# Reordered bank copies, splits, turns and a root in 8 steps in a hybrid RWKV-7 / gated-DeltaNet block

## What is computed

```python
xn = rmsnorm(x, norm_mix_pre);  p = xn @ w_in      # all projections of both branches
y_a = rwkv7(p);  y_b = gated_delta_rule(p)         # 32 heads of 64, 16 heads of 128, chunks of 64
mixed = sigmoid(p_gate_a) * y_a + sigmoid(p_gate_b) * y_b
x = x + rmsnorm(mixed @ w_out, norm_mix_post)
xn = rmsnorm(x, norm_ffn_pre)
hidden = silu(xn @ ffn_w_gate) * (xn @ ffn_w_up)   # width 5632
return x + rmsnorm(hidden @ ffn_w_down, norm_ffn_post)
```

## Time and profile before

| | us |
|---|---|
| median of 3 runs | 2201.25 (2199.06 to 2201.72) |
| the profiled execution | 2195.88 |
| its span, first to last instruction | 2194.2 |
| PE busy | 2091.8 (95%) |
| PE weight loads busy | 1804.8 (82%) |
| DVE busy | 1427.1 (65%) |
| ACT busy | 1086.2 (50%) |
| POOL busy | 160.2 (7%) |
| mean granted clock of PE | 0.987 |

### The profile page before, as it was taken

How to read it: one execution, slowest core, us unless ns; L and a number is a source line. 1 busy time by engine, 2 the same in 40 slices (tenths; PEclk the granted TensorE clock), 3 DMA queues, 4 the chain that set the end, 5 groups by cost and what they waited for, 6 DMA issues and landing times. The chain is left out here.

```text
span 2194.2 us, 49337 instructions
## 1 busy us (share of the span) xinstructions
PE 2091.8 (95%) x20515; PEld 1804.8 (82%) x20515; DVE 1427.1 (65%) x2868; ACT 1086.2 (50%) x2060; POOL 160.2 (7%) x277
## 2 busy tenths in 40 slices
PE   5999999999999999999999999799999999989997
PEld 5988888888888888888888888678888888878886
DVE  5568777777777877777777785754454444445445
ACT  4555555554655555555465554444444444434443
POOL 3010011011011011101101100000000000000000
PEclk9999999999999999999999999899999999999999
DMA  7655444454545444445454424545555555545553
GB/s 202 170 142 133 124 124 119 125 134 121 135 121 137 126 125 128 119 121 133 125 136 121 128 96 144 177 169 192 189 184 186 188 190 189 174 153 191 191 187 119
DMA packets 386941, 327.28 MB, mean 149 GB/s; under 512 B 11744, under 2 KB 334272, under 8 KB 380352
## 3 DMA queue, kind: packets, MB, share of 16 engines
q1 hardware_dynamic: 372688, 318.53, 49.4%
q10 hardware_dynamic: 14064, 6.04, 1.1%
HBM read 322.44 MB, written 2.10 MB: 148 GB/s over the span
## 5 line engine op out<-in xcount | busy, mean ns | idle before, releaser
L249 PE MATMUL ps<-hi_all,xh 128*128 128x384 f32 (+1 forms) x1568 | 564.1, 360 | 32.0 <-ACT pu L275 29.2
L498 DVE TENSOR_TENSOR lo_all<-stage,hi_all 128x1024 fp32r<-128x1024 f32 x263 | 322.2, 1225 | 365.9 <-ACT hi_all L494 365.6
L251 PE MATMUL ps<-hi_all,xl 128*128 128x384 f32 (+1 forms) x1568 | 531.7, 339 | 0.0
L250 PE MATMUL ps<-lo_all,xh 128*128 128x384 f32 (+1 forms) x1568 | 530.3, 338 | 0.0
L494 ACT ACTIVATE hi_all<-stage 128x1024 fp32r<-128x1024 f32 x260 | 275.5, 1060 | 416.1 <-PE ps L510 415.4
L244 DVE TENSOR_TENSOR lo_all<-stage,hi_all 128x768 fp32r<-128x768 f32 (+1 forms) x400 | 378.0, 965 | 120.2 <-ACT hi_all L239 119.5
L239 ACT ACTIVATE hi_all<-stage 128x768 fp32r<-128x768 f32 (+1 forms) x400 | 327.6, 833 | 216.4 <-PE ps L251 209.8
L249 PEld LDWEIGHTS ps<-hi_all,xh 128*128 128x128 f32 x1568 | 296.4, 189 | 67.9 <-ACT pu L275 36.4
L250 PEld LDWEIGHTS ps<-lo_all,xh 128*128 128x128 f32 x1568 | 297.4, 190 | 0.9
L251 PEld LDWEIGHTS ps<-hi_all,xl 128*128 128x128 f32 x1568 | 296.7, 189 | 0.9
L506 PE MATMUL ps<-hi_all,xh 128*128 128x512 f32 x704 | 277.2, 394 | 3.6 <-DVE lo_all L498 3.4
(11 more groups left out here) (280 smaller groups left out, 2656.8 us busy)
## 6 DMA issues: line engine op xcount, KB each, us to landing
stage<-in_w_in SPq DMA_DIRECT2D x288, 512.0 KB, 5.7
stage<-in_ffn_w_gate SPq DMA_DIRECT2D x44, 1024.0 KB, 5.2
stage<-in_ffn_w_up SPq DMA_DIRECT2D x44, 1024.0 KB, 5.1
stage<-in_ffn_w_down SPq DMA_DIRECT2D x22, 2048.0 KB, 7.4
stage<-in_w_out SPq DMA_DIRECT2D x16, 344.0 KB, 4.2
stage<-in_w_out SPq DMA_DIRECT2D x8, 516.0 KB, 4.9
stage<-in_w_in SPq DMA_DIRECT2D x8, 448.0 KB, 6.9
stage<-in_w_out SPq DMA_DIRECT2D x8, 336.0 KB, 4.0
```

The costliest lines, as they stand in the source:

```text
L249: nc.tensor.matmul(o, xh[:, kc, xs], high, start=kc == 0, stop=False)
L250: nc.tensor.matmul(o, xh[:, kc, xs], low, start=False, stop=False)
L251: return nc.tensor.matmul(o, xl[:, kc, xs], high, start=False, stop=kc == KC - 1)
L498: nc.vector.tensor_tensor(wlo[b], src, whi[b].bitcast(F32), ALU.subtract).then_inc(ffn_lo, 1)
```

## The change

`take_out(act, u, 2)` goes directly behind the copy `rhs` of chunk 2, and the two splits that stood before and after it go behind step (2,2); DVE does one split less ahead of the norms' sums and one more behind step (3,2). At the end of w_out DVE's sums go one ahead of the scales, ACT's first `stage_hi` goes from p = 5 to p = 2, and its `stage_lo` into the next block, behind `new_x(1)`. The first feed-forward block uses three buffers and may split two quanta ahead; PE turns each group one quantum later; the squares of the second norm are done at quanta 6 and 7. Behind the last block PE starts the first down step with bank pair 3, and `hidden`, `turn` and `store` of the last block lie within that step. At the end the banks come in order 2, 3, 1, 0 for both halves, each is squared and weighted by itself, and the results of t = 0 are made between the weighted products of t = 1. `root` replaces `rsqrt` in the feed-forward part: 8 steps, a column at a time, where the factor of each step is a per-partition scalar.

```diff
@@ -118,6 +118,39 @@
...
         step(nc.vector.scalar_tensor_tensor(y, t, 1.5, y, ALU.add, ALU.mult))
+def root_names(tag, columns):
+    return [f"{tag}{k}{c}" for k in ("y", "v", "t0", "z0", "t1", "z1", "t2", "z2") for c in range(columns)]
+def root(nc, dve, done, tag, y, v, w):
+    columns = y.shape[1]
+    def after(name):
+        dve.wait_ge(done.sem, done.after(name))
+    def at(x, c):
+        return x[:, c:c + 1]
+    for c in range(columns):
+        done.step(f"{tag}y{c}", nc.vector.tensor_scalar(at(y, c).bitcast(I32), at(v, c).bitcast(I32), -0.5, 1597463007.0,
+                                                        ALU.mult, ALU.add))
+    for c in range(columns):
+        done.step(f"{tag}v{c}", nc.vector.tensor_scalar(at(w, c), at(v, c), -0.5, None, ALU.mult))
+    for i in range(3):
+        for c in range(columns):
+            after(f"{tag}z{i - 1}{c}" if i else f"{tag}v{c}")
+            done.step(f"{tag}t{i}{c}", nc.vector.scalar_tensor_tensor(at(v, c), at(y, c), at(w, c), at(y, c),
+                                                                      ALU.mult, ALU.mult))
+        for c in range(columns):
+            after(f"{tag}t{i}{c}")
+            done.step(f"{tag}z{i}{c}", nc.vector.scalar_tensor_tensor(at(y, c), at(v, c), 1.5, at(y, c), ALU.add, ALU.mult))
+    for c in range(columns):
+        after(f"{tag}z2{c}")
...
@@ -487,10 +520,10 @@
...
-def stage_hi(act, n, b, src):
-    if not (isinstance(n, int) and n < 2):
-        act.wait_ge(ffn_used, n - 1)
+def stage_hi(act, n, b, src, ahead=1):
+    if not (isinstance(n, int) and n <= ahead):
+        act.wait_ge(ffn_used, n - ahead)
...
@@ -1158,7 +1191,7 @@
...
-def chunk_act(act, u, lag, k, c):
+def chunk_act(act, u, lag, k, c, between=None):
...
@@ -1168,6 +1201,8 @@
...
 fn(f"r{c}", rhs[:], ps[:, 4, 0:CH])
+if between:
+    between()
...
@@ -1265,11 +1300,12 @@
...
 fn("sqq", sq[:, 1:3, :], qkv[:, 0:2, :], ACT.Square)
-fill(1)
-chunk(1, 2)
-take_out(act, u, 2)
-fill(1)
+if prev:
+    chunk_act(act, u, 1, 1, 2, lambda: take_out(act, u, 2))
+else:
+    take_out(act, u, 2)
 chunk(2, 2)
+fill(2)
...
@@ -1351,7 +1387,8 @@
...
 for p in range(OP):
-    if p == OP - 1:
+    if p == 2:
...
@@ -1538,7 +1575,7 @@
...
 chunk(1, 2)
-fill(2)
+fill(1)
...
@@ -1663,8 +1700,9 @@
...
         fill(1)
-    out_scale_dve(dve, p)
-stage_lo(dve, 0, 0, ffn_quantum(0))
+    else:
+        out_scale_dve(dve, p - 1)
+out_scale_dve(dve, OP - 1)
...
@@ -1791,17 +1829,25 @@
...
 down_sum, down_square = sem("down_sum"), sem("down_square")
+B0 = (3, 0, 1, 2)
+LAST_B = (2, 3, 1, 0)
 A = Steps(sem("ffn_act"), [f"hi{g}" for g in G8] + ["ss0", "ss1"])
-V = Steps(sem("ffn_dve"), ["sum", "var"] + rsqrt_names("p") + ["x0", "x1"]
+V = Steps(sem("ffn_dve"), ["sum", "var"] + root_names("p", NT) + ["x0", "x1"]
           + [n for g in G8 for n in ([f"lo{g}", f"x{g + 2}"] if g < 6 else [f"lo{g}"])]
-          + ["v2"] + rsqrt_names("q") + ["half", "gate"]
-          + [n for t in range(NT) for n in [f"w{t}{b}" for b in (3, 2, 0, 1)] + [f"sum{t}", f"var{t}"] + rsqrt_names(f"r{t}_") + [f"y{t}0", f"y{t}1"]])
+          + ["v2"] + root_names("q", NT) + ["half", "gate"]
+          + [f"w0{b}" for b in LAST_B] + ["sum0", "var0"] + root_names("r0_", 1)
+          + ["w12", "y01", "w13", "y00", "w11", "w10", "sum1", "var1"] + root_names("r1_", 1) + ["y11", "y10"])
...
 QE = QD + NB * (JD - 1)
+def split_buffer(q, first):
+    return q % 3 if first else (q + 1) % 2
...
@@ -1830,7 +1876,7 @@
...
 for t in range(NT):
-    for h in range(2):
+    for h in (1, 0):
...
@@ -1853,14 +1899,14 @@
...
         act.wait_ge(ffn_landed[(q // 2) % 4], jb * 32 + 16 * (q // 8 + 1))
-    stage_hi(act, jb * QF + q, q % 2, ffn_quantum(q))
+    stage_hi(act, jb * QF + q, split_buffer(q, first), ffn_quantum(q), 2 if first else 1)
...
     high(q + 1)
-if first and q == 8:
-    for t in range(NT):
+if first and q in (6, 7):
+    for t in (q - 6,):
...
@@ -1879,20 +1925,22 @@
...
     block_act(jb, False)
-store(FB - 1)
-def down_act(j, s, n, landed):
+def down_act(j, s, n, landed, order=range(NB)):
...
         act.wait_ge(ffn_used, n - NB)
+    elif j == 0:
+        act.wait_ge(stored, FB - 1)
...
     act.wait_ge(down_in[s], landed)
-    for b in range(NB):
-        stage_hi(act, n + b, b % 2, down_quantum(s, b))
+    for i, b in enumerate(order):
+        stage_hi(act, n + i, (i + 1) % 2, down_quantum(s, b))
+down_act(0, 0, QD, 16, B0)
+store(FB - 1)
 act.wait_ge(stored, FB)
-for s in range(2):
-    down_act(s, s, QD + NB * s, 16)
+down_act(1, 1, QD + NB, 16)
...
@@ -1900,17 +1948,15 @@
...
 act.wait_ge(down_in[1], 8 * JD)
-for b in (2, 3, 0, 1):
+for b in LAST_B:
     if b < 2:
-        act.wait_ge(ffn_used, QE - 1 + b)
+        act.wait_ge(ffn_used, QE - b)
...
 for t in range(NT):
-    act.wait_ge(down_sum, t + 1)
-    for b in range(NB):
-        if t + b:
-            act.wait_ge(down_square, NB * t + b)
-        if b >= 2:
-            act.wait_ge(V.sem, V.after(f"w{t}{b}"))
+    for i, b in enumerate(LAST_B):
+        act.wait_ge(down_sum, NB * t + i + 1)
+        if t + i:
+            act.wait_ge(down_square, NB * t + i)
...
@@ -1942,7 +1988,7 @@
...
 done("v2")
-rsqrt(nc, dve, V, "q", 0, rr[:], ssx[:], rtm[:])
+root(nc, dve, V, "q", rr[:], ssx[:], rtm[:])
...
@@ -1951,7 +1997,7 @@
...
 if not (first and q == 0):
-    stage_lo(dve, jb * QF + q, q % 2, ffn_quantum(q))
+    stage_lo(dve, jb * QF + q, split_buffer(q, first), ffn_quantum(q))
...
@@ -1973,58 +2019,64 @@
...
 done("var")
-rsqrt(nc, dve, V, "p", 0, rr[:], ssx[:], rtm[:])
+root(nc, dve, V, "p", rr[:], ssx[:], rtm[:])
...
 new_x(1)
+stage_lo(dve, 0, 0, ffn_quantum(0))
...
     block_dve(jb, False)
-dve.wait_ge(gate_done, FB)
-hidden(FB - 1)
...
-def down_dve(j, s, n):
+def down_dve(j, s, n, order=range(NB)):
     left(j, s)
-    for b in range(NB):
-        stage_lo(dve, n + b, b % 2, down_quantum(s, b))
-for s in range(2):
-    down_dve(s, s, QD + NB * s)
+    for i, b in enumerate(order):
+        stage_lo(dve, n + i, (i + 1) % 2, down_quantum(s, b))
+        if isinstance(j, int) and j == 0 and i == 0:
+            dve.wait_ge(gate_done, FB)
+            hidden(FB - 1)
+down_dve(0, 0, QD, B0)
+down_dve(1, 1, QD + NB)
...
 left(JD - 1, 1)
-for i, b in enumerate((2, 3, 0, 1)):
+for i, b in enumerate(LAST_B):
...
+def weighted(t, b):
+    dve.wait_ge(down_square, NB * t + LAST_B.index(b) + 1)
+    cs = slice(CB * b, CB * b + CB)
+    V.step(f"w{t}{b}", nc.vector.tensor_tensor(y2[:, t, cs], ps[:, 2 * b + t, :], row[:, cs], ALU.mult))
+def result(t, h):
+    cs = slice(h * D // 2, (h + 1) * D // 2)
+    V.step(f"y{t}{h}", nc.vector.scalar_tensor_tensor(y2[:, t, cs], y2[:, t, cs], rr[:, t:t + 1], x2[:, t, cs],
+                                                     ALU.mult, ALU.add))
...
     one = slice(t, t + 1)
-    dve.wait_ge(down_sum, t + 1)
-    for b in (3, 2, 0, 1):
-        if b < 2:
-            dve.wait_ge(down_square, NB * t + b + 1)
-        cs = slice(CB * b, CB * b + CB)
-        V.step(f"w{t}{b}", nc.vector.tensor_tensor(y2[:, t, cs], ps[:, 2 * b + t, :], row[:, cs], ALU.mult))
-    dve.wait_ge(down_square, NB * t + NB)
+    for b in LAST_B:
+        weighted(t, b)
+        if t and b >= 2:
+            result(0, 3 - b)
...
     done(f"var{t}")
-    rsqrt(nc, dve, V, f"r{t}_", 0, rr[:, one], ssx[:, one], rtm[:, one])
-    done(f"w{t}1")
-    for h in range(2):
-        cs = slice(h * D // 2, (h + 1) * D // 2)
-        V.step(f"y{t}{h}", nc.vector.scalar_tensor_tensor(y2[:, t, cs], y2[:, t, cs], rr[:, one], x2[:, t, cs],
-                                                         ALU.mult, ALU.add))
+    root(nc, dve, V, f"r{t}_", rr[:, one], ssx[:, one], rtm[:, one])
+for h in (1, 0):
+    result(1, h)
...
@@ -2051,36 +2103,40 @@
...
                         if first and q < 8:
-                            for x in (range(3) if q == 0 else range(q + 2, min(q + 3, 8))):
+                            for x in (range(2) if q == 0 else [q + 1] if q < 7 else []):
...
                         kc = 2 * (q % (QF // 2))
-                        stage_mm(pe, jb * QF + q, q % 2, xh[:, kc:kc + 2, :], xl[:, kc:kc + 2, :],
+                        stage_mm(pe, jb * QF + q, split_buffer(q, first), xh[:, kc:kc + 2, :], xl[:, kc:kc + 2, :],
...
                     block_pe(jb, False)
-                turn(FB - 1)
-                pe.wait_ge(stored, FB)
-                def down_pe(j, s, n, first):
+                def down_pe(j, s, n, first, order=range(NB)):
                     pe.wait_ge(left_lo, j + 1)
-                    for b in range(NB):
-                        stage_mm(pe, n + b, b % 2, hh[s][:], hl[s][:], lambda t: ps[:, 2 * b + t, :], first
+                    for i, b in enumerate(order):
+                        if first and b == 0:
+                            pe.wait_ge(gate_done, FB)
+                        if first and b == 1:
+                            turn(FB - 1)
+                        if first and b == 2:
```

(12 more changed lines are left out.)

## The result

The changed kernel took 2160.52 us in the median of four runs (2159.42 to 2164.91); beside it the kernel before took 2200.15 (2193.41 to 2201.72). The ratio is 0.983 (0.9818 to 0.9843): 39.6 us less. The prediction was 2164, range 2157 to 2176.

The account below looks back on a forecast made before the run. TensorE was taken as the bound (2091.8 of 2194.2 us busy), so only its stops and slow clock matter. Terms summing to 37.4 us take the median from 2201.25 to 2164 us, range 2157 to 2176.

Parts of the forecast that it names:

- Unit loop: Units 1 to 14: TensorE's stop for the third `take_out` goes, net 0.85 us per unit, 11.9 us (8.4 to 13).
- the slack at `rhg`: VectorE's `rhg` ends barely before TensorE wants it: a stop of 0 to 0.15 us per unit, taken as 0.08.
- the "slower" rival: Unit loop: a late high part holds up `rhg`; from 2.7 us per unit it outweighs all gains; 2208 us at 3.2; chance 0.02.
- The clock: Units 1 to 14: all five clock falls at the stop vanish as the thin stretch shortens, 7.8 us (0 to 7.8).
- the clock falls stay: Units 1 to 15: poor stretches and other stops still lower the clock as often; 2174 us; chance 0.10.
- Unit 15: Last head unit: two stops go, the clock mostly recovers, less late `rhg`: 1.1 + 2.3 - 0.9 = 2.5 us (0 to 4).
- End of w_out, root, first block: From w_out's end into the first feed-forward block: hidden `stage_lo`, faster root, earlier first product; 3.0 us (1.5 to 4.5).
- the chain through turn, copy and low part: First feed-forward block: this chain paces each quantum despite the third buffer; stops of some 1.1 us at every other quantum.
- Last turn: Between last gate/up and first down products: pause goes, 5.65 us, and half clock behind it, 2.7; 8.3 us (7 to 8.6).
- end: After the last product: squares follow bank by bank, VectorE's last results come earlier; 2.9 us (2.3 to 3.2).
- The sum 24.95 + 1.4 + 1.2: At the last seam, `hidden` and the split of bank 0 end at 27.7 against 27.6: a stop of 0.15 us.
- The sum: Whole kernel: 1 + 11.9 + 7.8 + 2.5 + 3.0 + 8.3 + 2.9 = 37.4 us gained.

Follow-up runs that it names:

- ACT's move alone: The changed kernel with VectorE's splits in the unit loop as before, so only ScalarE's order is changed there: 2197.22 us, ratio 0.9991.
- the split first: The changed kernel with ScalarE's weight split ahead of the transposed group's copy in the first feed-forward block, second norm's squares later: 2154.12 us, ratio 0.9795.

## Why the prediction held, and where it didn't

*Unit loop.* The mechanism was right: the stop is gone, and 0.93 us per unit with it. The term was too small by 1.1 us, because the slack at `rhg` that I put at -0.08 was there: none of the units 1 to 14 shows a stop at the state products. What I had not seen is how much hangs on DVE's half of it. I named the late high part as the "slower" rival with 2.7 us per unit as its point of decision; ACT's move alone is close to this rival: a high part is late, though ahead of the norms and not of `rhg`, and it cost 1.85 us of stops per unit and four falls of the clock.

*The clock.* The size was right (5 x 1.56 us), the reason wrong. I took the length of the stretch of small products and standing, 3.4 to 2.45 us, as what decides. A stretch of 4.2 us without a stop shows no fall in 14 units, and one of 2.5 us with a stop of 0.85 shows five. The term came out because the change took the stop away too. Why five units and not all, with the same stop in each of 14, no run shows; the even distances of the falls are the only lead. The rival "the clock falls stay" was false in units 1 to 14 and true in unit 15.

*Unit 15* is the term that failed: 2.5 us predicted, -0.3 found. The two stops went, as foreseen, and a stop for `rhg` came, as foreseen too (0.6 and perhaps 0.3 predicted, 0.60 found; the profile calls it "issue", but DVE ended `rhg` at 1269.65). From the product at 1281.38 to the one at 1290.84 the kernel before took 9.46 us, the changed kernel 7.14 (1259.86 to 1267.00): 2.3 less, of which 1.1 is stops and 1.2 clock, where I had put 2.3 for the clock. The clock is the step that was too large, since the stop of 0.88 us ahead of the two stays, with a fall behind it. The rest went at the stop for `rhg` and at a place 40 us on that I had not looked at, with a second fall:

```profile
1259.86 0.21 PE L948 MATMUL ps<-headsel,early 128*32 128x2 f32 x5 [0.88 <-ACT early L1264]
...
1269.75 0.33 PE L948 MATMUL ps<-rhs,xit 64*64 64x64 f32 x4 [0.60 <-issue]
...
1303.78 0.40 PE L948 MATMUL ps<-yc,xs 32*32 32x16 f32 x27 [0.41 <-issue]
1305.51 0.37 PE L948 MATMUL ps<-yc,xs 32*32 32x16 f32 x21 [1.33 <-issue]
```
```profile
1269.29 0.36 DVE L1408 SCALAR_TENSOR_TENSOR rhg<-ps,nege,late 64x128 f32<-64x128 f32 x1
```
```profile
1306.00:1308.00 2.00, 2.00 (x8) 2.00 (x8) 1.32 (x3) 0.00 (x0) 0.00 (x0) 0.52 0.03 8
```

Inside one group of 48 small products PE stands 1.33 us and waits for nothing that this view shows; then its clock is 0.52. The kernel before has the stop too, 1.06 us and without a fall. In the other traces of this study it is 0.77, 0.77 and 0.79 (no fall), 0.92, 0.97, 0.99, 1.06, 1.06, 1.24, 1.24 and 1.25 (each with a fall) and 1.32 (none). It goes with no version, so the 1.8 us that the longer stop and its fall cost the changed kernel is put down to chance, not to the change. The DMA records give a lead to what PE stands for. They have a queue q8 of kind "instruction", packets of 16 KB; one of them lands at 1304.19 and PE goes on at 1305.51. In the kernel before it is 1327.13 and 1328.32. In each of the 14 traces PE goes on 1.2 to 1.5 us behind such a landing, and the later it lands against the last product ahead of the stop, the longer the stop tends to be. So it looks as if PE waits for its own instructions there; no run tests it.

*End of w_out, root, first block.* 3.8 us for 3.0. The end of w_out and the root gained 2.1 us for 1.45. The root took 1.87 us where I took 1.9. The surplus is in the sums ahead of the scales, which I had put at nothing: a scale used to start 0.90 us behind the sum that it needs (1405.72, 1406.62 in the kernel before) and now starts 0.78 behind another one, five times, 0.6 us in all. In the block I had put stops of 1.1 us at every other quantum and one of 2.4; they were three of 0.73 and one of 2.06, and none ahead of quantum 9. That the third buffer could not shorten them I put down to the chain through turn, copy and low part. That was wrong: the order of ACT's queue made them, and with the split first they vanish.

*Loop of the blocks.* I had nothing here, and it took 0.8 us more (44.83 us per block for 44.74). The buffers' new order is not the cause: with it other kernels of this study have 44.72 and 44.77, and the kernel with the old order 44.72. It is spread between executions.

*Last turn* and *end* came as worked out: 8.6 for 8.3 and 3.0 for 2.9. The sum 24.95 + 1.4 + 1.2 in the first is 27.55 and not 27.7, so that the stop of 0.15 us falls away; the trace has none there.

*The sum* is nearer than its terms: 35.9 us for 37.4 in the profiled executions, with terms that are off by 6 us if none is set against another. That -2.8 in unit 15 met +1.1 in the units and +0.8 at w_out is luck.

## What to carry to other kernels

When one engine's work is put behind another step, look at each engine that takes its product: its own queue has to move with it, or the wait only changes its name. Short stops of TensorE between small products can cost twice, once as stops and once as clock, so take first the one that the low clock follows in the windows. Where the profile says that an engine waited for nothing ("issue"), look at what the other engines and the DMA records end just before. And where an engine waits for two instructions on two banks, let it begin after the first.

## What the runs showed of the hardware

Granted clock: it fell to 1.2 GHz for a little over 3 us at stops of 0.85 and 0.89 us between small products in 5 or 6 of 14 units, two or three units apart; never at the stops of 0.47 us that come twice in each unit, never in 4.2 us of small products without a stop, and in none of 14 traces at a stop of 1.4 us between wide products.

VectorE: independent steps of one column start 0.07 us apart, dependent ones 0.18 to 0.26; one whose factor is a per-partition scalar lasts 0.22 us for 0.16.

TensorE: a standstill inside a run of small products, 0.77 to 1.33 us, at the same place of unit 15 in each trace and of another length in most. It ended 1.2 to 1.5 us after a packet of the "instruction" queue had landed, in all 14.
